# The layer-norm sums of seven channel tiles added on GpSimd, and the ones-matmuls cut from eight to two per sum

## The chip, the cores and the metric

The kernel runs on one core of a Trainium2 chip. The metric is the device time of one execution in microseconds (us). Besides TensorE (PE in the profile; PEld is its weight load), VectorE (DVE), ScalarE (ACT), GpSimd (POOL) and SyncE (SP, which here only issues loads) work side by side and are ordered by semaphores.

## The reference, cut to what matters

Two layers of a decoder are computed for 256 prompt tokens and 8 sequences of 8 sample tokens, so 320 token columns in all. The model width is 1024.

```python
def layer_norm(x, w, b):
    mu = jnp.mean(xf, -1, keepdims=True)
    var = jnp.mean(jnp.square(xf - mu), -1, keepdims=True)
    return (xf - mu) * lax.rsqrt(var + LN_EPS) * w + b

for l in range(DEPTH):                      # DEPTH = 2
    h = x * (1.0 + sc1) + sh1
    y, s_new, vn = token_mixer(h, ...)      # ends in the output projection w_out
    x = layer_norm(ALPHA * x + gt1 * y, ln1_w[l], ln1_b[l])
    h = x * (1.0 + sc2) + sh2
    f_out = swiglu(h, ...) if l == 0 else moe_swiglu(h, ...)
    x = layer_norm(ALPHA * x + gt2 * f_out, ln2_w[l], ln2_b[l])
```

There are four such layer norms over the width of 1024. A fifth kind, inside the token mixer over 512 values, is computed in another way and is not touched.

## The kernel before, in words

Activations lie channels-first: `xT` has 128 partitions, `KD = 8` channel tiles (numbered m) and 320 tokens. A sum over the channels is thus a sum over partitions and over the eight tiles. TensorE does both: it multiplies a 128x128 matrix of ones with each tile and accumulates the eight products in one bank. `shift` takes a rough mean from tile 0 alone; ScalarE writes it to `lnx` slot 2. `center` (VectorE, L1511) subtracts it from tile m and signals `dev_ready`. `squares` (ScalarE, L1193) writes the squares of tile m to `lnx` slot m % 2 and signals `sq_ready`; it may overwrite a slot once `sq_used` says that the squares of two tiles before were read. `sums` (TensorE) multiplies tile m (L727) and its squares (L731) with the ones. After tile 7, `deviation` computes mean and variance (ScalarE L1199, L1200, then VectorE L1525), and VectorE subtracts, takes the reciprocal and multiplies.

Everything is written out by hand, as one instruction stream per engine; nothing reorders it. The four layer norms stand at these places, which the text calls A, B, C and D:

- **A and C** (layer 0 and layer 1, after the output projection). TensorE works through eight output tiles, `half_out(j, 0)` and `half_out(j, 1)` with 24 matmuls in all, and after tile j it calls `sums(l, 0, j - 2)`. VectorE adds each tile to `xT` in `gated` (L1595, L1597, L1600), then centres the tile before it. `half_out(j)` waits for `wo_read(j - 2)`, which L1597 signals. VectorE also splits the next weight chunks (`make_lo`, L1487, 128x2048) and renews the sample states (`renew`, L1801, L1805) in this stretch, and GpSimd writes each renewed state out with a DMA (L557). `new_states` (L850) is TensorE's part in that. Tiles 6 and 7 are summed after the last projection.
- **B** (layer 0, after the dense feed-forward). TensorE works through the last down-projection chunk, eight tiles of 6 matmuls, and sums tile m - 4 after tile m; tiles 4 to 7 are summed after the last one. VectorE gates and centres each tile, and makes one weight chunk's low part (L1487) before `deviation`.
- **D** (layer 1, after the experts, at the end of the kernel). Nothing else runs: VectorE adds the experts' result (`add_channels`, L1606, L1607, L1609) and centres, ScalarE squares, TensorE sums all eight tiles, and the output follows.

GpSimd has little to do: masks at the start, the state loads and stores, and one `affine_select` on `wsT` in each layer (L540).

Of the kernel before, what the change touches and what calls it, by code (L numbers as in the profile page):

```python
# [5 lines left out]
ALU = mybir.AluOpType  # L6
# [6 lines left out]
P = 128  # L13
# [13 lines left out]
def hybrid_trunk(nc, x_prompt, x_sample, state_hgrn, c_prompt, c_sample, w_ada, b_ada, w_in, w_out,  # L27
# [4 lines left out]
    D = x_prompt.shape[2]  # L32
# [3 lines left out]
    T = TP + TS  # L36
    DEPTH = w_ada.shape[0]
    KD = D // P
# [74 lines left out]
    for w in range(NWIN - 4):  # L113
        a = PER * (w + 3)
        order += [("ada", a), ("ada", a + 1), ("w", w + 4), ("ada", a + 2), ("ada", a + 3)]
    a = PER * (NWIN - 4 + 3)
# [14 lines left out]
    with ExitStack() as ctx:  # L131
        def sb(name, shape, dt=F32, c=ctx):
            return c.enter_context(nc.sbuf_tensor(name, shape, dt))

        def signal(name, per=1, base=0):
            return Signal(ctx.enter_context(nc.semaphore(name)), per, base)
# [5 lines left out]
        xT = sb("xT", [P, KD, T])  # L142
        ident = sb("ident", [P, P])
        ones = sb("ones", [P, P])
# [30 lines left out]
        with ExitStack() as c1:  # L175
# [4 lines left out]
            k = sb("k", [P, H, T], c=c1)  # L180
# [24 lines left out]
        with ExitStack() as c2:  # L205
            accT = sb("accT", [P, KD, T], c=c2)
            tok_hi = sb("tok_hi", [P, NT, D], F32R, c=c2)
            tok_lo = sb("tok_lo", [P, NT - 1, D], F32R, c=c2)
            with ExitStack() as cx:
                sb("lnx_pad", [P, (NT * NE * P - 4 * T)], c=cx)  # L210
                lnx = sb("lnx", [P, 4, T], c=cx)
            G = sb("G", [P, NT, NE, P], F32R, c=c2)
            y_hi = sb("y_hi", [P, D], F32R, c=c2)
            y_lo = sb("y_lo", [P, D], F32R, c=c2)
            sil2 = sb("sil", [P, 2, 512], c=c2)
            aa2 = sb("aa", [P, 2, 512], c=c2)
            sil, aa = (a[:].rearrange("p c n -> p (c n)")[:, 0:2 * T] for a in (sil2, aa2))
            lg = sb("lg", [P, 8, NT, NE], c=c2)
            cmp = sb("cmp", [P, 2, NT, NE, NE], c=c2)
            red = sb("red", [P, 8, NT], c=c2)  # L220
            wslot = sb("wslot", [P, NE], c=c2)
            cnt = sb("cnt", [P, 16], c=c2)
            rounds_i = sb("rounds_i", [P, 1], I32, c=c2)
            with ExitStack() as c4:
                hf = sb("hf", [P, KD, T], c=c4)
            with ExitStack() as c4:
                xg1 = [sb("xg1_hi", [P, KD, 2 * P], F32R, c=c4), sb("xg1_lo", [P, KD, 2 * P], F32R, c=c4)]
            dT_hi, dT_lo = ([a[:, 0:2 * T].rearrange("p (j t) -> p j t", t=T) for a in pair]
                            for pair in ((y_hi, tok_hi[:, 0, :]), (y_lo, tok_hi[:, 1, :])))
# [86 lines left out]
        sh_ready = signal("sh_ready", 2)  # L316
        dev_ready = signal("dev_ready", 2 * KD)
        sq_ready = signal("sq_ready", 2 * KD)
        sq_used = signal("sq_used", 2 * KD)
        sum_mm = signal("sum_mm", 2)  # L320
        md_ready = signal("md_ready", 2)
        msq_ready = signal("msq_ready", 2)
# [79 lines left out]

        def moe_raw(i):
            return (MOE_RAW0 + i) % RAW

        def raw_slot(s):
            if s < RAW:
# [60 lines left out]
        def _(pool):  # L468
# [49 lines left out]
                                    channel_multiplier=0))  # L518
            link(pool.memset(eps[:, 0:1], LN_EPS))
            pool.memset(eps[:, 1:2], RMS_EPS).then_inc(consts.sem, 1)  # L520
            for l in range(DEPTH):

                if l == 0:
                    pool.wait_ge(hs_ready.sem, 1)
                else:
                    pool.wait_ge(x_ready.sem, x_ready.at(l - 1, 1))
                pool.dma_start(ws[:], a_ws[l].rearrange("h t s -> t h s")).then_inc(prep_in.sem, 16)
                pool.dma_start(bsr[:], a_bs[l:l + 1]).then_inc(prep_in.sem, 16)
                pool.dma_start(lnw, a_ln_w[l].partition_broadcast(P)).then_inc(prep_in.sem, 16)
                pool.dma_start(lnb, a_ln_b[l].partition_broadcast(P)).then_inc(prep_in.sem, 16)  # L530
                def state_in(h):
                    pool.dma_start(states[h], state_hgrn[l, :, h].rearrange("b d v -> d b v")).then_inc(st_in[h].sem, 16)

                if l:
                    state_in(0)
                    state_in(1)
                pool.memset(S[:], 0.0).then_inc(consts.sem, 1)

                pool.wait_ge(ws_read.sem, ws_read.at(l, 0))
                pool.affine_select(out=wsT[:], in_=wsT[:], compare_op=ALU.is_ge, fill=0.0, base=0,  # L540
                                   pattern=[[0, H], [1, P]], channel_multiplier=-1).then_inc(ws_masked.sem, 1)
                if l == 0:
                    pool.wait_ge(ada_used.sem, NALL)
                    state_in(0)
                    state_in(1)
                pool.wait_ge(vn_ready.sem, vn_ready.at(l))
                pool.dma_start(chunkv_prompt[l, 0], vtok[:, 1, :]).then_inc(cv_out.sem, 16)
                pool.dma_start(chunkv_sample[l].rearrange("b s a -> (b s) a"), vtok[0:TS, 2, :]).then_inc(cv_out.sem, 16)
                pool.wait_ge(lvl_done.sem, lvl_done.at(l, NL - 2))
                state_in(2)  # L550
                pool.wait_ge(qk_ready.sem, qk_ready.at(l))
                state_in(3)
                pool.wait_ge(sp_ready.sem, sp_ready.at(l, 1))
                pool.dma_start(st_prompt[l, 0].rearrange("h d v -> d h v"), stp).then_inc(sp_out.sem, 16)
                for h in range(H):
                    pool.wait_ge(st_new.sem, st_new.at(l, h))
                    pool.dma_start(st_sample[l, :, h].rearrange("b d v -> d b v"), states[h]).then_inc(st_out[h].sem, 16)  # L557
            pool.wait_ge(sp_out.sem, 16 * DEPTH)
            pool.wait_ge(cv_out.sem, 32 * DEPTH)
            for h in range(H):  # L560
                pool.wait_ge(st_out[h].sem, 16 * DEPTH)
            pool.wait_ge(x_ready.sem, x_ready.at(DEPTH - 1, 0))
            pool.memset(accT[:], 0.0).then_inc(sc_read.sem, 1)


        def loaded(eng, key):
# [32 lines left out]
        def sum_banks(i):  # L599

            return (bank[1], bank[2]) if i else (bank[7], bank[6])

        @block.tensor
        def _(pe):
# [116 lines left out]
            def sums(l, i, m):  # L721

                a, b = sum_banks(i)
                if m == 0:
                    pe.wait_ge(sh_ready.sem, sh_ready.at(l, i))
                pe.wait_ge(dev_ready.sem, dev_ready.at(l, KD * i + m))
                last = pe.matmul(a[:, 0:T], ones[:], xT[:, m, :], start=(m == 0), stop=(m == KD - 1))  # L727
                if m == KD - 1:
                    last.then_inc(sum_mm.sem, 1)
                pe.wait_ge(sq_ready.sem, sq_ready.at(l, KD * i + m))  # L730
                pe.matmul(b[:, 0:T], ones[:], lnx[:, m % 2, :], start=(m == 0), stop=(m == KD - 1)).then_inc(sq_used.sem, 1)  # L731


            def turn_x(n):

# [29 lines left out]
            for l in range(DEPTH):  # L765
# [25 lines left out]
                for t, t0, n in VTILES:  # L791
                    if t == 2:
                        pe.wait_ge(mx_read.sem, mx_read.at(l, 0))
                    b = bank[6 + t % 2]
# [161 lines left out]
            i = 0  # L956
# [1179 lines left out]
```

## Time and profile before

| | us |
|---|---|
| median of 3 runs | 1687.37 (1682.82 to 1691.3) |
| the profiled execution's own time | 1686.86 |
| its span, first to last instruction | 1685.1 |
| PE busy | 1566.8 (93%) |
| DVE busy | 1183.6 (70%) |
| ACT busy | 902.6 (54%) |
| POOL busy | 41.1 (2%) |

Busy time says how long an engine executed, not whether the end waited for it. The chain of waits tells the latter, and for a change at four small places the timeline of those places tells more than any total.

### The profile page before, as it was taken

How to read it: one execution, taken by the hardware profiler on the slowest of the kernel's cores; microseconds unless marked ns; L12 is line 12 of the kernel's file. 1: busy time of each engine (PE TensorE's matmuls, PEld its weight loads, DVE VectorE, ACT ScalarE, POOL GpSimd, SP SyncE). 2: the span in 40 equal slices, each digit the busy share in tenths (PEclk: the TensorE clock that was granted, in tenths of full speed). 3: DMA queues.
4: the chain of work that ended last, by engine and by line, in shares of the span. 5: the costliest groups of instructions: out<-in, count | busy, mean ns of one | idle time of the engine just before them, and what ended most of it. 6: DMA issues, size and time to landing. Idle time of an engine off the chain costs nothing.

```text
span 1685.1 us, 23549 instructions
## 1 busy us (share of the span) xinstructions
PE 1566.8 (93%) x9218; PEld 1343.1 (80%) x9218; DVE 1183.6 (70%) x1232; ACT 902.6 (54%) x822; POOL 41.1 (2%) x76
## 2 busy tenths in 40 slices
PE   6999988799999799886799999999999999999995
PEld 3778777699999699775778888888888888888873
DVE  2332447755556865666598988889788888988875
ACT  2544423433333456242377767677676766767653
POOL 2100010000000010000000000000000000000000
PEclk9899978999999899878699999999999999999997
DMA  9999844254444252231299999999999999999990
GB/s 315 326 338 313 281 139 127 80 158 150 149 148 146 75 171 99 60 107 51 75 326 361 359 309 354 335 363 350 309 358 339 364 340 319 357 341 365 331 333 32
DMA packets 242035, 415.10 MB, mean 246 GB/s; under 512 B 7891, under 2 KB 128893, under 8 KB 241926
## 3 DMA queue, kind: packets, MB, share of 16 engines
q1 hardware_dynamic: 238662, 402.31, 69.7%
q0 software_dynamic: 3264, 11.28, 2.3%
q8 instruction: 75, 1.23, 0.3%
q14 instruction: 34, 0.28, 0.0%
HBM read 406.75 MB, written 6.82 MB: 245 GB/s over the span
## 4 chain that ended last, share of the span: by engine, by line
PE 54%; DVE 4%; ACT 1%; issue 1%; DVEq 0%; ACTq 0%
PE bank L608 15%; PE bank L610 15%; PE bank L609 15%; PE bank L1035 1%; PE bank L997 1%; PE bank L611 1%; PE bank L612 1%; PE bank L613 1%; PE bank L1077 1%; PE bank L712 1%; PE bank L727 1%; PE bank L1078 1%; PE bank L952 1%; PE bank L731 0%; PE bank L963 0%
## 5 line engine op out<-in xcount | busy, mean ns | idle before, releaser
L1496 DVE TENSOR_TENSOR w_lo<-raw_ring,w_hi 128x2048 fp32r<-128x2048 f32 x264 | 604.5, 2291 | 110.9 <-ACT w_hi L1234 110.1
L1234 ACT ACTIVATE w_hi<-raw_ring 128x2048 fp32r<-128x2048 f32 x264 | 506.7, 1919 | 238.5 <-PE bank L610 238.5
L608 PE MATMUL bank<-w_hi,xg_hi 128*128 128x512 f32 (+1 forms) x768 | 294.1, 383 | 5.4 <-DVE xg_lo L1986 5.4
L610 PE MATMUL bank<-w_hi,xg_lo 128*128 128x512 f32 (+1 forms) x768 | 289.8, 377 | 0.0
L609 PE MATMUL bank<-w_lo,xg_hi 128*128 128x512 f32 (+1 forms) x768 | 289.5, 377 | 0.0
L611 PE MATMUL bank<-act_hi,w_hi 128*128 128x320 f32 x736 | 240.4, 327 | 33.2 <-DVE act_lo L1546 20.3
L612 PE MATMUL bank<-act_lo,w_hi 128*128 128x320 f32 x736 | 234.7, 319 | 0.0
L613 PE MATMUL bank<-act_hi,w_lo 128*128 128x320 f32 x736 | 234.3, 318 | 0.0
L1487 DVE TENSOR_TENSOR w_lo<-raw_ring,w_hi 128x2048 fp32r<-128x2048 f32 x65 | 148.7, 2288 | 103.0 <-ACT w_hi L1174 102.8
L611 PEld LDWEIGHTS bank<-act_hi,w_hi 128*128 128x128 f32 x736 | 145.6, 198 | 39.3 <-issue 30.6
L608 PEld LDWEIGHTS bank<-w_hi,xg_hi 128*128 128x128 f32 x768 | 145.2, 189 | 30.5 <-DVE xg_lo L1986 5.6
L610 PEld LDWEIGHTS bank<-w_hi,xg_lo 128*128 128x128 f32 x768 | 144.9, 189 | 29.0
L609 PEld LDWEIGHTS bank<-w_lo,xg_hi 128*128 128x128 f32 x768 | 145.4, 189 | 25.0
L1174 ACT ACTIVATE w_hi<-raw_ring 128x2048 fp32r<-128x2048 f32 x65 | 123.8, 1906 | 64.3 <-PE bank L613 61.1
L612 PEld LDWEIGHTS bank<-act_lo,w_hi 128*128 128x128 f32 x736 | 145.7, 198 | 0.6
L613 PEld LDWEIGHTS bank<-act_hi,w_lo 128*128 128x128 f32 x736 | 145.0, 197 | 0.0
L608 PE MATMUL bank<-w_hi,aT_hi 128*128 128x512 f32 x352 | 140.0, 398 | 1.0 <-DVE aT_lo L2007 1.0
L609 PE MATMUL bank<-w_lo,aT_hi 128*128 128x512 f32 x352 | 139.1, 395 | 0.0
L610 PE MATMUL bank<-w_hi,aT_lo 128*128 128x512 f32 x352 | 139.0, 395 | 0.0
L608 PEld LDWEIGHTS bank<-w_hi,aT_hi 128*128 128x128 f32 x352 | 66.1, 188 | 16.3 <-issue 1.2
L610 PEld LDWEIGHTS bank<-w_hi,aT_lo 128*128 128x128 f32 x352 | 66.1, 188 | 16.1
L609 PEld LDWEIGHTS bank<-w_lo,aT_hi 128*128 128x128 f32 x352 | 66.1, 188 | 14.8
(311 smaller groups left out, 2000.7 us busy)
## 6 DMA issues: line engine op xcount, KB each, us to landing
raw_ring<-in_e_gate_dram SPq DMA_DIRECT2D x90, 1024.0 KB, 5.2
raw_ring<-in_e_up_dram SPq DMA_DIRECT2D x90, 1024.0 KB, 5.3
raw_ring<-in_e_down_dram SPq DMA_DIRECT2D x88, 1024.0 KB, 5.0
raw_ring<-in_w_ada_dram SPq DMA_DIRECT2D x24, 1024.0 KB, 7.7
raw_ring<-in_w_in_dram SPq DMA_DIRECT2D x24, 1024.0 KB, 7.6
st<-in_w_ada_dram SPq DMA_DIRECT2D x12, 1024.0 KB, 8.5
kdsp<-in_w_ada_dram SPq DMA_DIRECT2D x12, 1024.0 KB, 9.6
raw_ring<-in_w_ff_gate_dram SPq DMA_DIRECT2D x11, 1024.0 KB, 5.4
```

Source lines behind the costliest of these rows:

```text
L608: pe.matmul(out, xh, wh, start=start, stop=False)
L609: pe.matmul(out, xh, wl, start=False, stop=False)
L610: return pe.matmul(out, xl, wh, start=False, stop=stop)
L611: pe.matmul(out, wh, xh, start=start, stop=False)
L612: pe.matmul(out, wh, xl, start=False, stop=False)
L613: return pe.matmul(out, wl, xh, start=False, stop=stop)
L712: last = pe.matmul(bank[3 + t][0:n, h * P:h * P + n], a[:, h, t0:t0 + n], b[:, h, t0:t0 + n], start=True, stop=True)
L727: last = pe.matmul(a[:, 0:T], ones[:], xT[:, m, :], start=(m == 0), stop=(m == KD - 1))
L1174: act.activation(w_hi[:, i % SPL, :], slot, ACT.Copy).then_inc(hi_ready.sem, 1)
L1234: act.activation(w_hi[:, (NSPLIT + i) % SPL, :], raw[:, s, :], ACT.Copy).then_inc(hi_ready.sem, 1)
L1487: dve.tensor_tensor(w_lo[:, i % SPL, :], raw_slot(landed["w", i][0]), w_hi[:, i % SPL, :].bitcast(F32), ALU.subtract).then_inc(lo_ready.se ...
L1496: dve.tensor_tensor(w_lo[:, r, :], raw[:, s, :], w_hi[:, r, :].bitcast(F32), ALU.subtract).then_inc(lo_ready.sem, 1)
```

## The change

GpSimd keeps two running sums, of the centred tiles and of the squares, over tiles 0 to 6: twelve additions of 128x320 per layer norm (`add_up`). TensorE then multiplies four things with the ones instead of sixteen: the two running sums, tile 7 and its squares. `shift` stays. The sums lie in the dead buffer `k` for A and C, and in a new part of memory (`pool_part`) for B and D. `sq_used` is now signalled by GpSimd's additions, and a new semaphore, `dv_added`, counts the additions of centred tiles.

```diff
+        dv_added = signal("dv_added", 2 * (KD - 2))
...
+            def add_up(l, i, m):
+
+                d, q2 = part_sums(i)
+                if m == 1:
+                    pool.wait_ge(dev_ready.sem, dev_ready.at(l, KD * i + 1))
+                    pool.tensor_tensor(d, xT[:, 0, :], xT[:, 1, :], ALU.add).then_inc(dv_added.sem, 1)
+                    pool.wait_ge(sq_ready.sem, sq_ready.at(l, KD * i + 1))
+                    pool.tensor_tensor(q2, lnx[:, 0, :], lnx[:, 1, :], ALU.add).then_inc(sq_used.sem, 2)
+                    return
+                pool.wait_ge(dev_ready.sem, dev_ready.at(l, KD * i + m))
+                pool.wait_ge(dv_added.sem, dv_added.at(l, (KD - 2) * i + m - 2))
+                pool.tensor_tensor(d, d, xT[:, m, :], ALU.add).then_inc(dv_added.sem, 1)
+                pool.wait_ge(sq_ready.sem, sq_ready.at(l, KD * i + m))
+                pool.wait_ge(sq_used.sem, sq_used.at(l, KD * i + m - 1))
+                pool.tensor_tensor(q2, q2, lnx[:, m % 2, :], ALU.add).then_inc(sq_used.sem, 1)
...
                 for h in range(H):
                     pool.wait_ge(st_new.sem, st_new.at(l, h))
                     pool.dma_start(st_sample[l, :, h].rearrange("b d v -> d b v"), states[h]).then_inc(st_out[h].sem, 16)
+                    if h:
+                        add_up(l, 0, 2 * h - 1)
+                        add_up(l, 0, 2 * h)
+                if l == 0:
+                    for m in range(1, KD - 1):
+                        add_up(l, 1, m)
...
             pool.memset(accT[:], 0.0).then_inc(sc_read.sem, 1)
+            for m in range(1, KD - 1):
+                add_up(DEPTH - 1, 1, m)
...
             def sums(l, i, m):
 
                 a, b = sum_banks(i)
+                d, q2 = part_sums(i)
                 if m == 0:
-                    pe.wait_ge(sh_ready.sem, sh_ready.at(l, i))
-                pe.wait_ge(dev_ready.sem, dev_ready.at(l, KD * i + m))
-                last = pe.matmul(a[:, 0:T], ones[:], xT[:, m, :], start=(m == 0), stop=(m == KD - 1))
+                    return
+                pe.wait_ge(sh_ready.sem, sh_ready.at(l, i))
+                if m == KD - 2:
+                    pe.wait_ge(dv_added.sem, dv_added.at(l, (KD - 2) * i + KD - 3))
+                    pe.matmul(a[:, 0:T], ones[:], d, start=True, stop=False)
                 if m == KD - 1:
-                    last.then_inc(sum_mm.sem, 1)
-                pe.wait_ge(sq_ready.sem, sq_ready.at(l, KD * i + m))
-                pe.matmul(b[:, 0:T], ones[:], lnx[:, m % 2, :], start=(m == 0), stop=(m == KD - 1)).then_inc(sq_used.sem, 1)
-
+                    pe.wait_ge(sq_used.sem, sq_used.at(l, KD * i + KD - 2))
+                    pe.matmul(b[:, 0:T], ones[:], q2, start=True, stop=False)
+                    pe.wait_ge(dev_ready.sem, dev_ready.at(l, KD * i + m))
+                    pe.matmul(a[:, 0:T], ones[:], xT[:, m, :], start=False, stop=True).then_inc(sum_mm.sem, 1)
+                    pe.wait_ge(sq_ready.sem, sq_ready.at(l, KD * i + m))
+                    pe.matmul(b[:, 0:T], ones[:], lnx[:, m % 2, :], start=False, stop=True).then_inc(sq_used.sem, 1)
```

On GpSimd, between layer 0's state store and layer 1's first loads, the kernel before has these rows (each is an instruction, written tile, read tile, shape, and the semaphores it waits for):

```order
L554 DMA out_dram<-kdsp 128x4x128 [waits sp_ready]
L557 DMA out_dram<-st 128x8x128 [waits st_new] x2
L557 DMA out_dram<-ze 128x8x128 [waits st_new] x2
L527 DMA ws<-in_a_ws_dram 128x4x128 [waits x_ready]
L528 DMA bsr<-in_a_bs_dram 1x16x32
```

The changed kernel has this at the same place, for layer norm A (`k` holds the two running sums):

```order
L582 DMA out_dram<-st 128x8x128 [waits st_new] x2
L535 TENSOR_TENSOR k<-xT 128x320 [waits dev_ready]
L537 TENSOR_TENSOR k<-lnx 128x320 [waits sq_ready]
L541 TENSOR_TENSOR k<-k,xT 128x320 [waits dv_added,dev_ready]
L544 TENSOR_TENSOR k<-k,lnx 128x320 [waits sq_used,sq_ready]
L582 DMA out_dram<-ze 128x8x128 [waits st_new]
L541 TENSOR_TENSOR k<-k,xT 128x320 [waits dv_added,dev_ready]
L544 TENSOR_TENSOR k<-k,lnx 128x320 [waits sq_used,sq_ready]
```

The two state stores from `ze` now stand behind additions that wait for centred tiles 2 and 4, and twelve more additions for B follow before the loads of layer 1.

On TensorE, at the end of the kernel (layer norm D), the kernel before has the shift's matmul and then eight pairs, of which two are shown:

```order
L719 MATMUL bank<-xT,ones 128x320 [waits z_ready]
L727 MATMUL bank<-xT,ones 128x320 [waits dev_ready,sh_ready]
L731 MATMUL bank<-lnx,ones 128x320 [waits sq_ready]
L727 MATMUL bank<-xT,ones 128x320 [waits dev_ready]
L731 MATMUL bank<-lnx,ones 128x320 [waits sq_ready]
```

The changed kernel has four matmuls behind the shift, and then the transposes of the output:

```order
L752 MATMUL bank<-xT,ones 128x320 [waits z_ready]
L763 MATMUL bank<-pool_part,ones 128x320 [waits sh_ready,dv_added]
L766 MATMUL bank<-pool_part,ones 128x320 [waits sq_used,sh_ready]
L768 MATMUL bank<-xT,ones 128x320 [waits dev_ready]
L770 MATMUL bank<-lnx,ones 128x320 [waits sq_ready]
L1188 MATMUL bank<-ident,xT 128x128 [waits y_ready]
```

All four now stand behind GpSimd's last additions; before, the first pair could start with the first centred tile.

## Rows read from the trace of the kernel before

**Rows 1.** The page: chain that ended last, shares by engine and line.
```profile
PE 54%; DVE 4%; ACT 1%; issue 1%; DVEq 0%; ACTq 0%
```
**Rows 2.** Waits between 750 and 812 us: engine, line, waited for, us, times, longest.
```profile
DVE xT L1595 <- PE bank L613: 10.8, 6, 3.3
DVE ze L1805 <- PE bank L850: 4.4, 1, 4.4
```
**Rows 3.** Timeline of layer norm C: start, us, engine, line, operation, tiles, shape, count.
```profile
777.22 0.70 PE L727 MATMUL bank<-xT,ones 128*128 128x320 f32 x2
777.76 0.70 PE L731 MATMUL bank<-lnx,ones 128*128 128x320 f32 x2
781.81 0.70 PE L727 MATMUL bank<-xT,ones 128*128 128x320 f32 x2
...
782.01 0.48 DVE L1595 SCALAR_TENSOR_TENSOR xT<-bank,modT,xT 128x256 f32<-128x256 f32 x1 [3.32 <-PE bank L613]
782.81 0.88 DVE L1511 TENSOR_TENSOR xT<-xT,lnx 128x320 f32<-128x320 f32 x2
...
786.13 0.49 DVE L1525 SCALAR_TENSOR_TENSOR nmean<-bank,lnx 128x320 f32<-128x320 f32 x1 [2.44 <-ACT lnx L1200]
```
**Rows 4.** Chain of waits at full clock in D: start, us, engine, line.
```profile
1665.36 0.54 PE bank L727 x2
1665.90 0.54 PE bank L731 x2
```
**Rows 5.** Timeline of layer norm A, VectorE alone.
```profile
297.86 2.29 DVE L1487 TENSOR_TENSOR w_lo<-raw_ring,w_hi 128x2048 fp32r<-128x2048 f32 x1 [0.73 <-ACT w_hi L1174]
300.07 1.22 DVE L1801 TENSOR_TENSOR ze<-ze,fe 128x1024 f32<-128x1024 f32 x1
308.31 2.29 DVE L1487 TENSOR_TENSOR w_lo<-raw_ring,w_hi 128x2048 fp32r<-128x2048 f32 x1 [0.73 <-ACT w_hi L1174]
```
**Rows 6.** Timeline of layer norm B, VectorE.
```profile
561.96 0.48 DVE L1511 TENSOR_TENSOR xT<-xT,lnx 128x320 f32<-128x320 f32 x1
566.87 0.23 DVE L1600 TENSOR_TENSOR xT<-xT,nmean 128x64 f32<-128x64 f32 x1
568.19 0.48 DVE L1595 SCALAR_TENSOR_TENSOR xT<-bank,modT,xT 128x256 f32<-128x256 f32 x1 [0.69 <-PE bank L613]
568.98 1.29 DVE L1511 TENSOR_TENSOR xT<-xT,lnx 128x320 f32<-128x320 f32 x3
570.18 2.28 DVE L1487 TENSOR_TENSOR w_lo<-raw_ring,w_hi 128x2048 fp32r<-128x2048 f32 x1
573.89 0.49 DVE L1525 SCALAR_TENSOR_TENSOR nmean<-bank,lnx 128x320 f32<-128x320 f32 x1 [1.43 <-ACT lnx L1200]
```
**Rows 7.** Timeline of layer norm D, VectorE and the end of TensorE's sums.
```profile
1656.82 0.48 DVE L1511 TENSOR_TENSOR xT<-xT,lnx 128x320 f32<-128x320 f32 x1
1657.23 0.42 DVE L1606 TENSOR_TENSOR hf<-accT,modT 128x256 f32<-128x256 f32 x1
1660.81 1.29 DVE L1511 TENSOR_TENSOR xT<-xT,lnx 128x320 f32<-128x320 f32 x3
1668.09 0.44 ACT L1199 ACTIVATE lnx<-bank 128x320 f32<-128x320 f32 x1 [1.08 <-PE bank L727]
1668.95 0.49 DVE L1525 SCALAR_TENSOR_TENSOR nmean<-bank,lnx 128x320 f32<-128x320 f32 x1 [6.85 <-ACT lnx L1200]
```
**Rows 8.** Stretches of B and D: length, then busy time and instructions by engine, PEclk, DMA share, GB/s.
```profile
576.00:580.00 4.00, 0.00 (x0) 0.00 (x0) 3.86 (x6) 1.77 (x3) 0.00 (x0) 0.65 0.23 77
...
1657.00:1660.00 3.00, 3.00 (x6) 1.63 (x6) 2.96 (x8) 1.68 (x5) 0.00 (x0) 0.50 0.00 0
1664.00:1668.00 4.00, 4.00 (x17) 2.81 (x16) 0.00 (x0) 1.41 (x3) 0.00 (x0) 1.00 0.00 0
1676.00:1679.00 3.00, 2.78 (x12) 2.26 (x12) 2.90 (x4) 1.97 (x5) 0.00 (x0) 0.50 0.00 0
```
**Rows 9.** Timelines of GpSimd and VectorE where GpSimd reads a tile.
```profile
69.87 2.29 DVE L1487 TENSOR_TENSOR w_lo<-raw_ring,w_hi 128x2048 fp32r<-128x2048 f32 x1 [12.10 <-ACT w_hi L1174]
71.26 1.40 POOL L540 TENSOR_SCALAR_AFFINE_SELECT wsT<-wsT 128x512 f32<-128x512 f32 x1 [21.54 <-ACT wsT L1275]
...
600.19 2.29 DVE L1487 TENSOR_TENSOR w_lo<-raw_ring,w_hi 128x2048 fp32r<-128x2048 f32 x1 [5.89 <-ACT w_hi L1174]
601.61 1.36 POOL L540 TENSOR_SCALAR_AFFINE_SELECT wsT<-wsT 128x512 f32<-128x512 f32 x1 [3.97 <-ACT wsT L1275]
```
**Rows 10.** GpSimd's short instructions at the start.
```profile
3.75 0.29 POOL L490 TENSOR_SCALAR_AFFINE_SELECT before<-ones 128x128 f32<-128x128 f32 x1
10.91 0.36 POOL L501 MEMSET keep<- 128x320 f32 x1
13.98 0.10 POOL L520 MEMSET eps<- 128x1 f32 x1
```
**Rows 11.** State stores, layer 0, and time from issue to landing.
```profile
304.25 0.89 POOL L557 DMA_DIRECT2D out_dram<-ze  x1 [9.57 <-DVE ze L1805]
...
DMA to landing us min/median/max: 3.8/3.9/5.0
```

More of the change, by code:

```diff
@@ L207, in hybrid_trunk @@
             tok_hi = sb("tok_hi", [P, NT, D], F32R, c=c2)
+            with ExitStack() as cx:
+                sb("pool_part_pad", [P, D + 2 * P], c=cx)
+                pool_part = sb("pool_part", [P, 2 * T], c=cx)
             tok_lo = sb("tok_lo", [P, NT - 1, D], F32R, c=c2)
@@ L404, in moe_raw, with part_sums @@
             return (MOE_RAW0 + i) % RAW
+        def part_sums(i):
+            flat = pool_part[:] if i else k[:].rearrange("p h t -> p (h t)")[:, 0:2 * T]
+            return flat[:, 0:T], flat[:, T:2 * T]
         def raw_slot(s):
```

## The prediction

> **What bounds the kernel.** I read the page first. The chain that ended last lies on TensorE for 54% of the span, and VectorE and ScalarE carry 4% and 1% [rows 1]; the rest of the chain is small pieces. So time taken from TensorE's stream is worth something where TensorE is what the others wait for, and the four layer norms must be read one by one in their timelines.
>
> In C, VectorE's gating (L1595) waited for the projection's last matmul six times, 10.8 us in all, and its renewal of a state waited 4.4 us for TensorE [rows 2]. TensorE is the bound there. From one tile's sums to the next is 781.81 - 777.22 = 4.59 us [rows 3], of which the two ones-matmuls are 0.54 + 0.53 = 1.07 us at full clock (chain of waits, [rows 4]) and the projection 3.52 us. In B the first matmuls of the sums also hold up gating (0.69 us before L1595), the last centring ends at 568.98 + 1.29 = 570.27 us, and the variance step L1525 starts only at 573.89 us, behind TensorE's sums [rows 6]. In D the last centring ends at 1662.10 us and L1525 starts at 1668.95 us [rows 7]: there too the sums are the bound, slowed at first by a granted clock of 0.50 (1.2 GHz), later 1.00 (2.4 GHz) [rows 8].
>
> **What an addition costs.** No row shows a GpSimd addition of this size. A write alone of 128x320 took 0.36 us [rows 10], the lower bound. GpSimd's `affine_select` of 128x512 took 1.40 and 1.36 us, the upper bound, though 128x128 took only 0.29 us [rows 10]. Both long ones began while VectorE ran a 128x2048 subtraction with two inputs in SBUF, and ended 72.66 - 72.16 = 0.50 us and 602.97 - 602.48 = 0.49 us after that subtraction's end [rows 9]. I read this as: GpSimd could not read until VectorE's two-input instruction was over, and then needed 0.50 us for 512 columns, 0.97 ns each. An addition reads two operands; one after the other that is 2 x 320 x 0.97 ns = 0.62 us, and with 0.10 us for the smallest instruction [rows 10] 0.72 us. I take 0.75 us.
>
> The Trainium skill ("SBUF — State Buffer", "Who interferes with whom") says that a VectorE instruction with two SBUF inputs contends with a GpSimd instruction that reads SBUF, and that whichever comes first holds the shared ports for the whole instruction. By that rule, the trace agrees for the one direction that it shows. The same skill ("GPSIMD Engine Reference", "3.1 Elementwise — side-by-side cycle accounting") gives 2.6 cycles an element for an addition; an estimate from it is 0.69 us plus dispatch, close to the value taken, so the sum would be the same.
>
> **What this does to each place.** Twelve additions are 12 x 0.75 = 9.0 us of GpSimd, 1.5 us a tile. Where VectorE's two-input instructions run in the same stretch, the two add up.
>
> *C.* Five pairs (tiles 0 to 4) leave TensorE's stream ahead of the last projection tile: 5 x 1.07 = 5.35 us. Before, from the last projection matmul (781.8) to L1525 (786.13) were 4.3 us. Now VectorE gates and centres tiles 6 and 7 until 1.9 us after that matmul (782.81 + 0.88, [rows 3]); two additions for tile 6 follow (1.5 us, the centring of tile 7 holds the port until then), then the matmuls of the square sum, tile 7 and its squares (3 x 0.54 = 1.6 us) and the usual step of 0.4 us: 5.4 us. C gains 5.35 - 1.1 = 4.2; I take 4.0 us for small waits.
>
> *A.* The same, but VectorE has two weight halves of 2.29 us and a renewal of 1.22 us in this stretch [rows 5], which become what the projection waits for once TensorE is 1 us a tile quicker, and each of them can be held up by an addition or hold one up. Following the stream: `half_out(6)` waits for L1597 of tile 4, which stands behind the subtraction (now from 298.3), an addition and the renewal, and starts near 304.5 instead of 307.2; the last projection matmul is 3.7 us earlier; the tail is longer as in C. A gains 2.8 us. The state stores are issued later, behind the additions for tiles 2 and 4: the last, now at 304.25, near 311.8. It lands 3.8 to 5.0 us after issue [rows 11], by 317, and what waits for it (`modulate`) comes at about 320. It is hidden by 3 us; were it not, the loss would be the excess alone. Additions for tiles 5 and 6 queue behind that store's 0.89 us, which is included. Squares (ScalarE) now wait for an addition two tiles back; at 4 us a tile that costs nothing here.
>
> *B.* Centring of tile 1 ends at 562.44 us, and the first addition starts. TensorE no longer delays VectorE, but GpSimd wants 1.5 us a tile and VectorE 0.63 us a tile of two-input work (L1600 0.23, L1511 0.4 from start to start). Serialised: 9.0 us, plus 3.2 us for VectorE's remaining two-input pieces (six centrings, four additions of the sample part), plus 2.28 us for the weight half (L1487), which stands ahead of the last additions or of L1525: the last square sum is ready at 562.4 + 14.5 = 577, rounded up by the starts' gaps to 577.4. TensorE has then done nothing for over 10 us. Before, the clock was down to 0.65 on average within 576 to 580 with the last matmul over at 573.4 [rows 8], so the matmuls run at 1.07 us each: sum of tile 6 done before, then three matmuls, 3.2 us, and 0.3 us to L1525: 581.0 against 573.89. B loses 7.1 us.
>
> *D.* From the centring of tile 1 (end 1657.30) VectorE has 4.8 us of work without a gap until 1662.10, all with two SBUF inputs [rows 7]. Serialised with 9.0 us of additions: 1671.1. TensorE is at the low clock, as it was at 1676 after 7 us with little to do [rows 8]: three matmuls 3.2 us, the step 0.4 us: L1525 at 1674.7 against 1668.95. D loses 5.7 us.
>
> The sum: -2.8 + 7.1 - 4.0 + 5.7 = +6.0 us. The profiled execution took 1686.86 us, so 1692.9 us; the median is 0.5 us higher: 1693 us. What follows each layer norm is TensorE's, VectorE's and ScalarE's chain as before, so a shift passes on whole.
>
> **The ends of the unknown.** At 0.36 us an addition, B's last sum waits only for VectorE (-1.4 us) and D loses 1.1 us: 1680 us in all. At 1.36 us, 24 additions in B and D cost 14.6 us more and A and C about 2: 1710 us. The value lies nearest the 0.50 us row, doubled for two operands.
>
> **Rivals.**
> 1. *No exclusion between additions and VectorE.* Then B's and D's additions run at 0.8 us one after the other: in B to 572.1, in D to 1667.0 us; four matmuls at the low clock follow, partly hidden. L1525 comes at 575.7 (+1.8) and 1670.6 (+1.7); A and C gain 4.1 and 4.2: net -4.8, 1682 us. For it: no row shows VectorE itself held up. Against it: the two ends at 0.5 us after the subtraction. Chance 0.17.
> 2. *Additions with handover cost 1.0 us or more (the slower side).* Each addition must take the port back from VectorE, wait for two semaphores, and its writes must land. 24 x 0.25 = 6 us more in B and D, 1 us in A and C: 1700 us. It decides the sign of a measurable loss from about 0.85 us an addition on. Chance 0.23.
> 3. *A's and C's gain goes into VectorE's or the store's waits*: up to 6.8 us more, 1700 us. For it: the weight halves in A; against: C has none late in its stretch and 10.8 us of VectorE's waits to spare. Chance 0.06.
> 4. *Cheap additions* near 0.4 us: 1680 us. Chance 0.04.
> The forecast has 0.50.
>
> A measurement of this kernel tells about 0.5%, 8.4 us, from no change: 1678.9 to 1695.8. The forecast lies inside on the slow side; a fifth of it and rivals 2 and 3 lie above. Faster 0.05, same 0.57, slower 0.38. The range must hold rival 1 and reach rival 2: 1682 to 1702 us.
>
> **What would show it.** In the changed profile: an addition's start-to-start distance of 0.75 us alone and more beside L1511 or L1609; L1511 and L1609 in D spaced over 0.8 us instead of 0.4; L1525's counterpart in D about 18 us after the first centring instead of 13; three ones-matmuls of 1.07 us at clock 0.50 in B and D; no gap in A and C ahead of the projection's tiles but that of tile 6 in A. The prediction is wrong if additions take half or double that time, if VectorE's instructions keep their spacing, or if TensorE's clock stays up in B and D (each 1.6 us less).

## The result and the profile after

The change made the kernel slower by 0.7%: 1697.79 us (median, 1695.58 to 1703.7) against 1687.03 us, ratio 1.0068 with a 95% interval of [1.0049, 1.0086]. The forecast was 1693 us. The profiled execution took 1695.71 us, its span 1694.0 us (before 1686.86 and 1685.1 us).

The page of the changed kernel, busy time and the chain that ended last. Before, the chain read as in [rows 1]:
```profile
PE 1543.8 (91%) x9122; PEld 1325.3 (78%) x9122; DVE 1199.7 (71%) x1232; ACT 902.6 (53%) x822; POOL 91.4 (5%) x124
PE 53%; DVE 4%; issue 2%; ACT 1%; POOL 1%; DVEq 0%; ACTq 0%; POOLq 0%
```
The shares hardly move. What they hide shows place by place, in the timelines: from the first centring of a layer norm (L1511 before, L1549 after) to the step that forms the variance (L1525 before, L1563 after). Each number below is the difference of two start times on VectorE; the last column runs from that step in D to the end of the span. The change's total is the sum of its row less that of before.

| us | A | B | C | D | D's step to the end |
|---|---|---|---|---|---|
| before | 31.35 | 13.12 | 31.35 | 12.93 | 16.15 |
| changed | 31.23 | 20.06 | 29.28 | 18.18 | 16.92 |
| difference | -0.1 | +6.9 | -2.1 | +5.3 | +0.8 |

That is +10.8 us, as much as the medians differ by. (The two spans differ by 8.9 us only; the stretches outside these places vary by a few us from execution to execution of one kernel, from the start to A above all: 288.3 us before, 286.3 after.)

In A and C one more split helps: the stretch up to VectorE's last gating (L1595 before, L1633 after), which starts when TensorE's last projection matmul is done, and the tail behind it.

| us | A, to the last gating | A, tail | C, to the last gating | C, tail |
|---|---|---|---|---|
| before | 27.23 | 4.12 | 27.23 | 4.12 |
| changed | 23.27 | 7.96 | 21.99 | 7.29 |

TensorE did become 4.0 and 5.2 us earlier, and the tails took nearly all (A) and most (C) of it back.

The tail of C in the changed kernel, from its timeline (start, us, engine, line, operation, tiles, shape, count, wait before):
```profile
782.23 0.48 DVE L1633 SCALAR_TENSOR_TENSOR xT<-bank,modT,xT 128x256 f32<-128x256 f32 x1 [2.24 <-PE bank L646]
783.02 0.89 DVE L1549 TENSOR_TENSOR xT<-xT,lnx 128x320 f32<-128x320 f32 x2
783.59 1.04 POOL L541 TENSOR_TENSOR k<-k,xT 128x320 f32<-128x320 f32 x1 [1.80 <-DVE xT L1549]
784.59 0.85 POOL L544 TENSOR_TENSOR k<-k,lnx 128x320 f32<-128x320 f32 x1
784.77 1.40 PE L763 MATMUL bank<-k,ones 128*128 128x320 f32 x2 [2.58 <-POOL k L541]
785.97 1.27 PE L766 MATMUL bank<-k,ones 128*128 128x320 f32 x2
787.03 1.27 PE L768 MATMUL bank<-xT,ones 128*128 128x320 f32 x2
788.10 1.27 PE L770 MATMUL bank<-lnx,ones 128*128 128x320 f32 x2
789.52 0.49 DVE L1563 SCALAR_TENSOR_TENSOR nmean<-bank,lnx 128x320 f32<-128x320 f32 x1 [5.61 <-PE bank L770]
```
And two stretches of the same, by windows (length, then busy time and instructions of PE, PEld, DVE, ACT, POOL, then PEclk, DMA share, GB/s):
```profile
782.00:786.00 4.00, 1.42 (x5) 0.82 (x4) 1.64 (x5) 0.87 (x2) 1.86 (x2) 0.77 0.00 0
786.00:790.00 4.00, 3.38 (x7) 1.65 (x5) 0.48 (x2) 0.77 (x2) 0.00 (x0) 0.50 0.00 0
```
TensorE waits 2.58 us for the last addition. In that wait its granted clock falls: over the four us from 786 on it is 0.50, that is 1.2 GHz, and the ones-matmuls start 1.20, 1.06 and 1.07 us apart where [rows 3, 4] have 0.54. Two moments are to be read together: all four multiplications are still to do when the last addition begins, and they are done at half speed.

The tail of A has nearly the same picture, only that the clock is back before the fourth ones-matmul (0.72 us at 316.49), and one thing more:
```profile
308.79 0.90 POOL L582 DMA_DIRECT2D out_dram<-ze  x1
309.61 0.48 DVE L1633 SCALAR_TENSOR_TENSOR xT<-bank,modT,xT 128x256 f32<-128x256 f32 x1 [0.28 <-PE bank L646]
309.72 0.87 POOL L541 TENSOR_TENSOR k<-k,xT 128x320 f32<-128x320 f32 x1
310.26 1.23 DVE L1638 TENSOR_TENSOR xT<-xT,nmean 128x64 f32<-128x64 f32 x1
313.15 1.40 PE L763 MATMUL bank<-k,ones 128*128 128x320 f32 x2 [3.58 <-POOL k L541]
...
316.49 0.72 PE L770 MATMUL bank<-lnx,ones 128*128 128x320 f32 x2
```
GpSimd issues a state store for 0.90 us first, so the additions for tile 5 meet VectorE's L1638, an instruction of 0.23 us that now shows as 1.23 us.

B, where the weight half L1525 (L1487 before, [rows 6]) runs:
```profile
570.57 2.94 DVE L1525 TENSOR_TENSOR w_lo<-raw_ring,w_hi 128x2048 fp32r<-128x2048 f32 x1
571.32 2.90 POOL L541 TENSOR_TENSOR pool_part<-pool_part,xT 128x320 f32<-128x320 f32 x1
574.19 0.85 POOL L544 TENSOR_TENSOR pool_part<-pool_part,lnx 128x320 f32<-128x320 f32 x1
574.37 1.41 PE L763 MATMUL bank<-pool_part,ones 128*128 128x320 f32 x2 [11.54 <-POOL pool_part L541]
579.12 0.49 DVE L1563 SCALAR_TENSOR_TENSOR nmean<-bank,lnx 128x320 f32<-128x320 f32 x1 [5.61 <-PE bank L770]
```
And D, part of the timeline of VectorE and GpSimd, and its end:
```profile
1658.90 0.49 DVE L1549 TENSOR_TENSOR xT<-xT,lnx 128x320 f32<-128x320 f32 x1 [1.21 <-ACT lnx L1226]
...
1663.01 1.03 POOL L541 TENSOR_TENSOR pool_part<-pool_part,xT 128x320 f32<-128x320 f32 x1 [0.76 <-DVE xT L1549]
1663.26 1.14 DVE L1549 TENSOR_TENSOR xT<-xT,lnx 128x320 f32<-128x320 f32 x1
1664.01 1.10 POOL L544 TENSOR_TENSOR pool_part<-pool_part,lnx 128x320 f32<-128x320 f32 x1
1664.32 1.08 DVE L1647 SCALAR_TENSOR_TENSOR xT<-accT,modT,xT 128x256 f32<-128x256 f32 x1
1665.08 1.04 POOL L541 TENSOR_TENSOR pool_part<-pool_part,xT 128x320 f32<-128x320 f32 x1
...
1671.34 0.86 POOL L541 TENSOR_TENSOR pool_part<-pool_part,xT 128x320 f32<-128x320 f32 x1
1672.15 0.86 POOL L544 TENSOR_TENSOR pool_part<-pool_part,lnx 128x320 f32<-128x320 f32 x1
1672.34 1.40 PE L763 MATMUL bank<-pool_part,ones 128*128 128x320 f32 x2 [13.94 <-POOL pool_part L541]
...
1677.08 0.49 DVE L1563 SCALAR_TENSOR_TENSOR nmean<-bank,lnx 128x320 f32<-128x320 f32 x1 [6.42 <-PE bank L770]
```
Alone, an addition takes 0.86 us and the next starts 0.81 to 0.84 us later. Side by side with VectorE, additions start 1.04 us apart, and VectorE's centrings and gatings, 0.40 us apart in [rows 7], are 1.0 us apart and last 1.08 to 1.14 instead of 0.48 us. Both engines look busy at the same time; the length of the rows is partly waiting.

### The profile page after: what moved, and what is told of

Same layout as the page of the kernel before. It is cut to its first block, busy times and chain, and to the rows that moved or that the text cites. A ratio compares the mean times of both kernels' runs of the same rounds, so it can differ in the third digit from the quotient of the medians.

```text
span 1694.0 us, 23458 instructions
## 1 busy us (share of the span) xinstructions
PE 1543.8 (91%) x9122; PEld 1325.3 (78%) x9122; DVE 1199.7 (71%) x1232; ACT 902.6 (53%) x822; POOL 91.4 (5%) x124
## 4 chain that ended last, share of the span: by engine, by line
PE 53%; DVE 4%; issue 2%; ACT 1%; POOL 1%; DVEq 0%; ACTq 0%; POOLq 0%
PE bank L641 15%; PE bank L643 14%; PE bank L642 14%; PE bank L1073 1%; PE bank L1035 1%; PE bank L1115 1%; PE bank L745 1%; PE bank L1116 1%; PE bank L990 1%; PE bank L1001 0%; PE bank L644 0%; PE bank L1100 0%; DVE xT L1574 0%; PE bank L645 0%; PE bank L646 0%
## 5 line engine op out<-in xcount | busy, mean ns | idle before, releaser
L1525 DVE TENSOR_TENSOR w_lo<-raw_ring,w_hi 128x2048 fp32r<-128x2048 f32 x65 | 150.6, 2318 | 103.0 <-ACT w_hi L1212 102.8
L641 PEld LDWEIGHTS bank<-w_hi,aT_hi 128*128 128x128 f32 x352 | 66.1, 188 | 16.1 <-issue 1.2
```

The costliest lines, as they stand in the source:

```text
L641: pe.matmul(out, xh, wh, start=start, stop=False)
L1525: dve.tensor_tensor(w_lo[:, i % SPL, :], raw_slot(landed["w", i][0]), w_hi[:, i % SPL, :].bitcast(F32), ALU.subtract).then_inc(lo_ready.se ...
```

## The experiments

Call a layer norm "on GpSimd" when its tiles are added up there. The times are medians. The first four kernels ran on one chip beside the kernel before at 1687.35 us, the next four beside it at 1687.66 us, the last two beside it at 1687.84 us.

**A and C alone on GpSimd, and B and D alone.** Two kernels; the other two layer norms are summed on TensorE as before.
```diff
 def sums(l, i, m):
+    if i not in ON:            # ON = (0,) for A and C, (1,) for B and D
+        ... as in the kernel before
+        return
```


> GpSimd sums tiles 0 to 6 only in A and C; B and D are summed on TensorE as in the kernel before. My theory: the two projections do run shorter (4.0 and 5.2 us up to the gating of tile 7), but the tail behind them is longer by 3.8 and 3.2 us, because two additions stand in it and the four ones-matmuls run at half clock after the wait. The change's traces give A -0.1 and C -2.1 us, so about 1685 us, 0.1% below before (0.999). Rival, that the later state stores or something else of A and C carries the loss: above 1687 us, with a wait on a store in the trace.

> GpSimd sums tiles 0 to 6 only in B and D; A and C as in the kernel before. My theory: all of the loss is here, 6.9 us in B, 5.3 in D and 0.8 in the output's transposes at the low clock: about 1700 us, ratio 1.0077. Rival, that the loss is spread over the whole kernel (slower execution through longer GpSimd use): about 1692 us.

Measured: A and C alone 1686.16 us, ratio 0.9988 [0.9975, 1.0001]; B and D alone 1701.86 us, ratio 1.0089 [1.0074, 1.0104]. By places, A and C alone have 31.55, 13.12, 29.27, 12.61 and 16.16 us (2.2 us less than before); B and D alone 31.35, 20.06, 31.35, 18.18 and 16.92 us (13.0 us more). So the loss is in B and D, and the +0.8 us at the end comes with D. Each place behaves as in the changed kernel but for A, 31.55 instead of 31.23 us: here the fourth ones-matmul still ran at the low clock. The gain in A and C, 6.8 us forecast, is 2.2 us in the changed kernel and 1.9 us here, and the timing can hardly tell this kernel from the one before. Where the gain went is what the next two ask about.

**TensorE kept busy.** The changed kernel with matmuls of the ones with themselves, 128 columns into a free bank, ahead of TensorE's wait for the last additions.
```diff
                 if m == KD - 2:
+                    for _ in range({(0, 0): 14, (1, 0): 12, (0, 1): 44, (1, 1): 52}[l, i]):
+                        pe.matmul(bank[3 if i else 5][:, 0:P], ones[:], ones[:], start=True, stop=True)
                     pe.wait_ge(dv_added.sem, ...)
```


> The changed kernel, with matmuls of ones by ones into a free bank (14 in A, 44 in B, 12 in C, 52 in D, each 128 columns) put ahead of TensorE's wait for the additions, so that it is busy while it waits. They add work and compute nothing that is used. My theory: the granted clock stays at 1.00, the four ones-matmuls take 0.54 us each instead of 1.07 in all four places (2.1 us each, 8.5 us in all, 0.5 to 1 us more from the output's transposes): about 1689 us. Rival, the additions alone make the tails and the clock is a side effect: 1698 us, or later if the added matmuls outlast the additions.

Measured: 1695.74 us, ratio 1.005 [1.0035, 1.0065]. The places: A 29.84, B 19.67, C 27.57, D 16.51, end 16.92 us, against 31.23, 20.06, 29.28, 18.18 and 16.92. D's ones-matmuls, from the timeline of this kernel, now 0.54 to 0.78 us apart (1.06 to 1.20 us in the changed kernel):
```profile
1674.38 0.70 PE L777 MATMUL bank<-pool_part,ones 128*128 128x320 f32 x2
1675.16 0.78 PE L780 MATMUL bank<-pool_part,ones 128*128 128x320 f32 x2
1675.78 0.70 PE L782 MATMUL bank<-xT,ones 128*128 128x320 f32 x2
1676.32 0.70 PE L784 MATMUL bank<-lnx,ones 128*128 128x320 f32 x2
```
The window around them, in the same kernel:
```profile
1672.00:1676.00 4.00, 3.92 (x28) 3.25 (x28) 0.67 (x1) 0.57 (x2) 3.02 (x4) 1.00 0.00 0
```
The clock therefore costs the changed kernel 1.4 us in A, 1.7 in C and 1.7 in D. In B the extra matmuls ended 1.65 us before the additions, the ones-matmuls behind this wait were slow again, and only 0.4 us came back. The end of the kernel kept its 16.92 us: the clock fell again after these matmuls. So the theory held in three places of four and for 5.2 of its 8.5 us; of the rival, that the additions alone make the tails, what is left is the part that did not come back. The timing alone does not show the gain: the intervals of the two ratios overlap. Nor are the places exact. Each is read from one execution, and with the same code D took 17.66 to 18.18 us, or 12.53 to 12.93 us where TensorE sums it, partly by where the clock returned.

**The running sums multiplied earlier.** A and C: tiles 0 to 5 on GpSimd, both sums multiplied right behind the last projection tile, tiles 6 and 7 on TensorE. B and D are summed on TensorE, as before the change.
```diff
-                if m == KD - 2: d ...          # 7 tiles on GpSimd
-                if m == KD - 1: q2, xT 7, squares 7
+                if m == 5: d, q2               # 6 tiles on GpSimd
+                if m >= 6: xT m, squares m
```


> As ac_only, but GpSimd sums only tiles 0 to 5 in A and C; TensorE multiplies the two running sums right behind the last projection tile and then tiles 6 and 7 and their squares. My theory: no addition is left in the tail of C, little in that of A, and TensorE has too little idle time for its clock to fall: A -2.6, C -5.2, about 1679 us, ratio 0.9955. Rival, that the projection's gain is given back whatever the tail (VectorE or ScalarE late): 1685 us like ac_only.

Measured: 1677.19 us, ratio 0.994 [0.9927, 0.9953]; the places 28.41, 13.11, 26.08, 12.55 and 16.13 us, 8.6 us less than before, 8.2 of them in A and C. The tail of C in this kernel:
```profile
775.81 0.70 PE L770 MATMUL bank<-k,ones 128*128 128x320 f32 x2
776.35 0.70 PE L772 MATMUL bank<-k,ones 128*128 128x320 f32 x2
777.35 0.81 PE L776 MATMUL bank<-xT,ones 128*128 128x320 f32 x2 [0.29 <-DVE xT L1559]
779.07 0.70 PE L780 MATMUL bank<-lnx,ones 128*128 128x320 f32 x2
780.13 0.49 DVE L1573 SCALAR_TENSOR_TENSOR nmean<-bank,lnx 128x320 f32<-128x320 f32 x1 [2.43 <-ACT lnx L1248]
```
The two running sums now fill the time in which TensorE used to wait for VectorE's last gating and centrings; the last wait is 0.29 us; the clock stays up and C's tail is 4.12 us, as before the change. C keeps the whole 5.3 us of TensorE's work, and the theory (A -2.6, C -5.2 us) held with -2.9 and -5.3 us.

**What of an addition excludes VectorE.** Two kernels, both the change with its additions replaced: by a memset of the same tile (a write, no read) and by a copy of the new tile (one read, one write). Neither forms the sums.
```diff
-pool.tensor_tensor(d, d, xT[:, m, :], ALU.add)
+pool.memset(d, 1.0)                     # the first kernel
+pool.tensor_copy(d, xT[:, m, :])        # the second
```


> The changed kernel with each of GpSimd's additions replaced by a memset of the same 128x320 tile: it writes and reads nothing, all waits and signals stay, the sums are not computed. My theory, that VectorE's instructions with two SBUF inputs and GpSimd's reads exclude each other: VectorE's centring in D is back at 0.48 us each and 0.40 us apart, its weight half in B at 2.28 us; a memset takes 0.36 us; D from first centring to variance about 11 us instead of 18.2. Rival, that any GpSimd instruction of this rate (its semaphores, its writes) slows VectorE: centring stays over 1 us in D.

> The changed kernel with each addition replaced by a copy of the new tile into the running sum's place: one read and one write of 128x320, waits and signals kept, the sums are not computed. My theory: one read is enough for the exclusion, so VectorE's centring in D is stretched by about the copy's own time (0.4 to 0.5 us alone), to 0.8 to 0.9 us, and the copy beside the weight half in B takes over 2 us; D from first centring to variance about 14 us. Rival, that only GpSimd's two-operand reads collide: VectorE as in the kernel before.

Measured: with memsets the whole took 3349.9 us, with three times as many expert matmuls (2304 instead of 768 in each of the three largest groups), presumably because the wrong sums send tokens to other experts; only the places can be compared. With copies it took 1680.93 us, one execution. D in the first, then in the second:
```profile
3324.50 0.48 DVE L1561 TENSOR_TENSOR xT<-xT,lnx 128x320 f32<-128x320 f32 x1
3324.74 0.36 POOL L546 MEMSET pool_part<- 128x320 f32 x1
3324.90 0.47 DVE L1659 SCALAR_TENSOR_TENSOR xT<-accT,modT,xT 128x256 f32<-128x256 f32 x1
```
```profile
1653.44 0.73 DVE L1561 TENSOR_TENSOR xT<-xT,lnx 128x320 f32<-128x320 f32 x1
1653.78 0.71 POOL L546 COPY pool_part<-lnx 128x320 f32<-128x320 f32 x1
1654.10 0.67 DVE L1659 SCALAR_TENSOR_TENSOR xT<-accT,modT,xT 128x256 f32<-128x256 f32 x1
...
1656.98 0.45 POOL L543 COPY pool_part<-xT 128x320 f32<-128x320 f32 x1
```
A GpSimd instruction that only writes leaves VectorE alone: 0.48 us, 0.40 apart, as before. One that reads one tile already excludes it: the copy takes 0.45 us alone and 0.64 or 0.71 beside VectorE, and VectorE's 0.48 becomes 0.73 (0.8 to 0.9 expected). In B the weight half takes 2.29 us beside memsets, and a copy beside it 2.51 us. D from centring to variance step: 10.77 us with memsets, 13.70 with copies, 18.18 with additions, 12.93 before.

The two kernels also show something on the clock that they were not built for. In C, TensorE's ones-matmuls behind the last wait, with copies and then with memsets:
```profile
775.86 0.78 PE L775 MATMUL bank<-k,ones 128*128 128x320 f32 x2 [2.17 <-POOL k L543]
776.48 0.70 PE L778 MATMUL bank<-k,ones 128*128 128x320 f32 x2
```
```profile
773.33 1.39 PE L775 MATMUL bank<-k,ones 128*128 128x320 f32 x2 [1.88 <-POOL k L543]
774.51 1.27 PE L778 MATMUL bank<-k,ones 128*128 128x320 f32 x2
```
Behind the longer wait the clock stayed at 1.00 (the tail is 4.88 us), behind the shorter one it was 0.50 until the fourth matmul (6.26 us). The length of the wait alone does not decide.

**Five tiles instead of six, and two tiles in B.**
```diff
-                if m == 5: d, q2               # as in the kernel two above
+                if m == 5: d, q2               # 5 tiles on GpSimd, tiles 5 to 7 on TensorE
```


> As the kernel with the first six tiles on GpSimd in A and C, but with the first five: TensorE has d and q2 at once behind the last projection tile, then three tiles. My theory: the tail of A loses the wait for GpSimd's fifth pair (1 us shorter than with six), the tail of C gets one pair more (0.6 us longer, since TensorE is the bound there until tile 6): together the same within 1 us, 1677 us, ratio 0.994. Rival, fewer GpSimd instructions are better everywhere: 1675 us.

> Six tiles on GpSimd in A and C, tiles 0 and 1 in B (two additions), D on TensorE. My theory: in B the two additions are over before TensorE has finished the down-projection's tiles, and TensorE has one pair less and no wait for the table load of the first square, so B from first centring to variance is 11.5 us instead of 13.1: 1675.5 us, 1.5 us under the kernel with A and C alone. Rival, even two additions cost B as much as they save through VectorE's stretched centring: no difference.

Measured: five tiles 1676.82 us, ratio 0.9937 [0.992, 0.9955], C 26.60 instead of 26.08 us, A 27.88 instead of 28.41: five and six tiles can't be told apart by time. With six tiles in A and C and tiles 0 and 1 of B on GpSimd (D on TensorE) 1675.77 us, ratio 0.9924 [0.9907, 0.9942], the lowest median here, though its interval overlaps with those of the two kernels before it; B took 12.00 us instead of 13.12 (11.5 expected). The 1.1 us lie ahead of B's last gating, where TensorE has one pair less; the two additions stretched one L1648 (0.48 us) and one centring (1.16 us).

**The state store behind the additions.** The changed kernel, and the version with two tiles in B, each with GpSimd's last state store of a layer issued behind the last additions.
```diff
                 for h in range(H):
+                    if h == H - 1:
+                        add_up(l, 0, 5); add_up(l, 0, 6)
                     pool.wait_ge(st_new.sem, st_new.at(l, h))
                     pool.dma_start(st_sample[l, :, h] ...)
```


> The changed kernel with one thing moved: in each layer GpSimd's last state store is issued behind the additions for tiles 5 and 6 instead of ahead of them. In the changed kernel the store started at 308.79 us, took 0.90 us, and pushed the addition for tile 5 into VectorE's L1638 (0.23 us elsewhere, 1.23 us there). Theory: this store is why A's tail (last gating to variance step) is 7.96 us and C's only 7.29 us; moved behind, A's tail is near 6.9 to 7.3 us, A's whole stretch near 30.4 us instead of 31.23, and C, B and D keep 29.3, 20.1 and 18.2 us; the time is about 1 us less, which the timing can't tell. Rival: the tail of A is set by the addition for tile 6, which waits for VectorE's last centrings anyway; then A stays within 0.2 us of 31.2. A second rival: the store now lands too late and the modulation waits for it; then the stretch from A's variance step to B grows by some us.

> The best version so far (six tiles on GpSimd in A and C, tiles 0 and 1 in B, D on TensorE: 1675.77 us, A 28.42 us) with the last state store of each layer issued behind the addition for tile 5. Theory of the store: A's tail falls from 5.16 to about 4.1 us, A to 27.4 us, the whole by 1.0 us to about 1674.8 us, ratio near 0.992. Rival (the store costs nothing in the tail): A stays at 28.4 us. Third case, the store lands late and something waits for it: A's gain is given back between A and B.

Measured: 1697.03 us, ratio 1.0065 [1.0045, 1.0086], and 1677.06 us, ratio 0.9936 [0.9919, 0.9953]. A takes 30.80 instead of 31.23 us in the first, 28.11 instead of 28.42 in the second; from there to B next to nothing changes (241.46 against 241.49 us in the first, 241.18 against 240.93 in the second), so the later store harms nothing that the places show. The timing tells neither kernel from the one without the move. A's tail in the first, from the timeline:
```profile
311.20 0.86 POOL L541 TENSOR_TENSOR k<-k,xT 128x320 f32<-128x320 f32 x1 [0.57 <-DVE xT L1552]
312.02 0.86 POOL L544 TENSOR_TENSOR k<-k,lnx 128x320 f32<-128x320 f32 x1
312.05 0.90 DVE L1641 TENSOR_TENSOR xT<-xT,nmean 128x64 f32<-128x64 f32 x1
313.43 1.04 POOL L541 TENSOR_TENSOR k<-k,xT 128x320 f32<-128x320 f32 x1 [0.56 <-DVE xT L1552]
```
The last addition ends 3.89 us after A's last gating starts, 4.21 us before the move. So the store cost 0.3 us, less than the 0.7 to 1.0 us that the theory gave it; the other 0.1 us of A comes from the clock, which returned a little earlier. The additions for tile 5 still meet VectorE's L1641, which now shows 0.90 us instead of 1.23. Neither the theory nor its rival (0.2 us at most) held in full.

## Why the prediction was right or wrong

The total lay between the forecast's 1693 and the 1700 us of rivals 2 and 3, inside the range, but the change cost 10.8 us where the sum had 6.0. By its steps:

- **TensorE earlier in A and C: right.** 3.7 and 5.35 us forecast, 3.96 and 5.24 us measured (27.23 less 23.27 and 21.99).
- **B and D: right**, 7.1 and 5.7 us forecast, 6.9 and 5.3 us measured, in part by luck: their parts were off both ways. The last sum came 16.6 us after B's first centring by the forecast (577.4 less 560.8) and 16.0 us by the trace; in D 15.1 and 14.1 us. Full serialisation was a little too strict, by more than the longer additions cost: an addition (0.83 us from start to start alone) and a VectorE instruction (0.40 us) together took 1.04 us. Against that, four matmuls and not three followed the last sum, since the one of the running sum of centred tiles starts only 0.67 us before the last addition ends and takes 1.20 us: from last sum to variance step 4.1 us in both instead of the 3.6 us forecast.
- **Exclusion of GpSimd's reads and VectorE's two-input instructions: right**, and in both directions. The row of [rows 9] had shown one direction only, and rival 1 (0.17) fell. The memset and the copy narrow it down to GpSimd's reads. The Trainium skill ("SBUF — State Buffer", "Who interferes with whom"), on which the prediction had leaned, says that a VectorE instruction with two SBUF inputs contends with a GpSimd instruction that reads SBUF, and not with one that only writes it. The traces agree: an addition that starts beside VectorE at 1664.01 us ends only at 1665.11, 0.7 us after VectorE's centring (ended 1664.40), the weight half in B holds an addition for 2.90 us, and the memset changed nothing.
- **An addition at 0.75 us: too low by a tenth**, 0.81 to 0.84 us from start to start. So rival 4 (0.4 us) fell, and rival 2, which had asked for 1.0 us, had its 1700 us near the total without its mechanism: the 1.04 us in D hold VectorE's instruction too.
- **The tails of A and C: wrong, and this is the step that failed.** "5.4 us" in C, with "the matmuls of the square sum, tile 7 and its squares (3 x 0.54 = 1.6 us)", is 5.2 us as the table counts, since the last gating starts 0.2 us later than the forecast's count; it was 7.29 us. A's tail, "longer as in C", was 7.96 us. So A gained 0.1 us instead of 2.8, C 2.1 us instead of 4.0. In C the last addition ended where the forecast had it, 3.4 us after the last projection matmul. The part behind it was mis-sized: 1.6 + 0.4 = 2.0 us forecast, 4.1 us measured (785.44 to 789.52), because the matmuls ran 1.06 us apart and the first of the four, which fits in front at full clock, did not. The prediction gave B and D the low clock and A and C the full one, because TensorE had been busy there until the tail. It did not ask what the clock does in the new wait of 2.6 us (3.6 us in A) that the change itself puts in front of these matmuls. Kept busy, TensorE gave back 1.7 of C's 1.9 us and 1.4 of A's 2.7 us. Of A's other 1.3 us, 0.3 us is the store ahead of the additions of tile 5; the rest (VectorE's pieces stretched by these additions) is read from the rows only and is not shown by a run. Rival 3 (0.06) had the gain of A and C lost in waits of VectorE or the store; 4.6 us of it were lost, but 3.1 of them came back when TensorE was kept busy.
- **The end: left out.** Both batches of output transposes take 2.8 us, at clock 0.50, where before the second took 1.55 us: +0.8 us. The end was 16.86 to 16.92 us in every kernel with D on GpSimd and 16.1 to 16.2 us in those without, but for the one with five tiles (17.34 us; its transposes took 1.53 us as well, and the extra 1.2 us lie behind ScalarE's last copy, where only the output's last stores, issued by SyncE, were still under way). Keeping TensorE busy up to D's ones-matmuls did not bring it back. Why the clock rises later stays open, as does why it stayed up behind the copies' wait of 2.17 us.

Together, 2.7 + 1.9 + 0.8 less 0.2 and 0.4 us are the 4.8 us between the +6.0 forecast and the +10.8 us found.

## What to carry to other kernels

Work taken off TensorE paid here where what replaced it was over before TensorE ran dry: cut the moved share so that its result is consumed in a gap that was there anyway (in A and C six of eight tiles, multiplied right behind the last projection tile, gained 0.6% where seven tiles gained 0.1% or nothing). Before giving GpSimd element-wise work, list VectorE's instructions with two SBUF operands in the same stretch: where these are dense and at the end of a chain, as in B and D, the two engines' times nearly add up. And when a change makes TensorE wait, cost the matmuls behind the wait at the low clock too: here that came true behind the waits of 1.65 us and more that the rows show, but not behind the 2.17 us in A and C of the copies' kernel.

## What the runs showed of the hardware

- Behind a wait of 2.6 us in C, matmuls ran 1.06 us apart at clock 0.50 instead of 0.54 us at 1.00; behind 1.88 us in C with memsets they ran 1.07 to 1.18 us apart, behind 1.65 us in B of the kernel with extra matmuls 0.91 to 1.07 us. Behind 2.17 us, in A and in C with copies, they ran 0.53 to 0.62 us apart at 1.00. Before the change, with a wait of 0.29 us ahead of them, the last ones-matmuls of A were 0.54 us apart, and the clock was 1.00 from 318 to 322 us.
- GpSimd's instruction of 128x320 took 0.36 us (memset), 0.45 us (copy) and 0.86 us (addition) alone. One write, one read and one write, two reads and one write are not in proportion: from memset to copy it is 0.09 us, from copy to addition 0.41 us. How much of that is the second read and how much the arithmetic is not shown.
- The gating of A, with one operand in a bank, did not contend: it kept 0.48 us (L1633 at 309.61), and the addition that began during it took 0.87 us. The same operation in D, with `accT` from SBUF in the bank's place (L1647), took 1.08 us beside additions. VectorE's 128x64 addition with two SBUF operands went from 0.23 to 1.23 us.
